# Feed-forward blocks of a two-stack transformer: up and down chunks interleaved, up chunks as seven products in every other iteration

## The chip, the cores and the metric

The kernel runs on one core of a Trainium2 chip. The metric is device time in microseconds (us) for one execution of the whole program. The engines of the core work in parallel, each with an in-order queue of its own: TensorE (PE, matmuls; PEld is its weight load), VectorE (DVE), ScalarE (ACT), GpSimd (POOL) and SyncE (SP), which here only issues DMAs. They wait for each other through semaphores.

## The reference

512 tokens of width 1024 pass through a first block (token mixers, memory attention, a feed-forward block with a convolution over the tokens) and two layers of a second block (feed-forward, mixer, feed-forward). The change is in the five feed-forward blocks (FFNs), which are

```python
def conv_ffn(n, w_up, conv_w, conv_b, w_down):       # FFN 0
    u, g = jnp.split(n @ w_up, 2, axis=-1)
    gp = jnp.pad(g, ((0, 0), (pad, pad), (0, 0)))
    gc = sum(gp[:, j:j + S] * conv_w[j] for j in range(CONV_WIDTH)) + conv_b
    return (jax.nn.silu(gc) * u) @ w_down

def swiglu(x, w_gate, w_up, w_down):                 # FFN 1 to 4
    return (jax.nn.silu(x @ w_gate) * (x @ w_up)) @ w_down
```

with `D_MODEL = 1024`, `D_FF = 2816`, all in float32. Each is applied to a normed input and its result, times 1.0 or 0.5, is added to the stream `h`.

## The kernel before

**Precision.** Every float32 product is made of three matmuls (L1995 to L1997, `products`): high part by high part, high weight by low input, low weight by high input. ScalarE makes the high part of a weight chunk (`split_hi`, L508, `w_hi` from `stage`), VectorE the low part (`split_lo`, L1002, `w_lo`). Activations are split in the same way (`x_hi`, `x_lo`; `f_hi`, `f_lo`).

**Chunks.** All weights come as one stream of chunks of 128 x 2048 values (1 MB), in the order in which TensorE uses them. `stage`, `w_hi` and `w_lo` have two slots each, for even and odd chunks. ScalarE splits chunk c + 2 when chunk c is done (`chunk_done`), VectorE follows (`lo_ready`), and SP loads chunk c + 4 into the slot that this frees. TensorE begins a chunk when its `lo_ready` and the evacuation of older PSUM tiles (`acc_evac`) are there.

**An FFN before.** The 2816 hidden columns are 22 tiles of 128, two to an iteration, so 11 iterations. Iteration `it` has a gate chunk (256 columns of w_gate) and an up chunk (256 of w_up). The iterations fall in three parts (`PARTS`: 4, 4 and 3 iterations); after each part come four chunks of w_down, each for 256 of the 1024 output columns with the part's 8, 8 or 6 tiles as the contraction. The tiles of gate, up and down lie in PSUM banks 0 to 3 in turn; banks 4 to 7 hold five of the products below.

**Eight and seven products.** A gate chunk is a 2 x 2 block product (contraction in halves, columns in two tiles, tokens in halves). As eight products it is 48 matmuls of 512 columns (`eight`). As seven products of sums (`seven_products`, a Strassen-Winograd scheme) it is 84 matmuls of 256 columns. For it VectorE makes four sums of the weights (`gate_sums`, `s_f`), ScalarE and VectorE split them (`s_hi`, L517; `s_lo`, L1012), and once an FFN four sums of the input: ScalarE scales (`t_half`), VectorE adds (`token_sums`, L1066 to L1071), both split (`t_hi`, `t_lo`). VectorE then puts the products together, in part while the chunk runs (`gate_early`, L1034 to L1043) and in part after it (`gate_evac`, L1054 to L1059). In FFN 0 the gates 4 to 10 are done so, in the others the gates 2 to 10. Up chunks are always eight products.

**VectorE's order in an iteration before.** It evacuates the gate (`gate_evac`; L1051 for eight products), splits the next gate chunk (`gate_lo(i, it + 1)`), does the convolution in FFN 0 (L1126 to L1130), then the token sums (all in iteration 0, in FFN 0 two each in iterations 0 and 1), evacuates the up tiles (L1140), splits the next up chunk, makes weight sums, `f_lo` (L1150) and the early part of the next gate. ScalarE applies silu (L576, L579) and makes `f_hi` (L561), GpSimd multiplies gate and up (L1873).

**Between FFNs.** `residual` adds the last four chunks of down to `h` (L1093) and makes `x_hi` (L544) and `x_lo` (L1099); GpSimd sums the squares (L1849, L1851). TensorE runs gate 0 of the next FFN, then a matmul with ones for the norm (L2035, for FFN 1 L2040), ScalarE takes the root (L531) and VectorE the reciprocal, `rstd` (L1080). Only then can gate 0 be evacuated, while TensorE runs up 0.

Of the kernel before, what the change touches and what calls it, by code (L numbers as in the profile page):

```python
# [19 lines left out]
F32 = mybir.dt.float32  # L20
# [7 lines left out]
P = 128  # L28
# [23 lines left out]
PARTS = [("a", 0, 4), ("b", 4, 4), ("c", 8, 3)]  # L52
SEVEN_FROM = [4, 2, 2, 2, 2]
NONE_OF = FT // 2


def _down_name(i, part):

    return f"down{i}" if part == "c" else f"down{i}{part}"


def _ffn(i):

    return [phase for part, _, n in PARTS for phase in ((f"up{i}{part}", 2 * n, 4 * n), (_down_name(i, part), 4, 8))]

# [66 lines left out]
def build(nc, stream, x_in, mem_in, pos_in, par_in, const_in, out):  # L132
    ctx = ExitStack()
    with ctx:
# [50 lines left out]
        snap = place("snap", ROPE, [P, 3, HALF])  # L185
# [103 lines left out]
        def sem(name):  # L289
# [24 lines left out]
        seven_done, seven_snap, seven_sum = sem("seven_done"), sem("seven_snap"), sem("seven_sum")  # L314
# [17 lines left out]
        side_landed, mem_sq_ready, side_stat, side_std, mem_n, mem_hi_ready, mem_ready = (  # L332
            sem("side_landed"), sem("mem_sq_ready"), sem("side_stat"), sem("side_std"), sem("mem_n"), sem("mem_hi_ready"), sem("mem_ready"))
# [54 lines left out]
        def nth(i, it):

            return sum(NONE_OF - first for first in SEVEN_FROM[:i]) + it - SEVEN_FROM[i]  # L390

        def gate_chunk(i, it):

            part, base, _ = PARTS[it // 4]
            return C0[f"up{i}{part}"] + 2 * (it - base), T0[f"up{i}{part}"] + 4 * (it - base)

        def seven_at(p, t=None):

            bank, half = PRODUCT[p] if p in PRODUCT else ((t + p - 3) % 4, 0)
            return ps[:, bank, HALF * half:HALF * half + HALF]  # L400
# [5 lines left out]
        T_GROUPS = {i: {0: [0, 1], 1: [2, 3]} if i == 0 else {0: [0, 1, 2, 3]} for i in range(5)}  # L406
        T_ROUND_AT = {i: 1 if i == 0 else 0 for i in range(5)}
# [89 lines left out]
        def _(act):  # L497
# [12 lines left out]
            def gate_hi(i, it):  # L510

                c, _ = gate_chunk(i, it)
                if not seven(i, it):
                    return split_hi((c, 0))
                split_hi((c, 0), SINGLES)
                act.wait_ge(s_sum, 4 * nth(i, it) + 4)
                act.activation(s_hi[:, :], s_f[:, :], ACT.Copy).then_inc(s_rounded, 1)  # L517

            def first_product(n):

                act.wait_ge(seven_done, 4 * n + 1)
# [11 lines left out]
            def residual(name):  # L533
# [3 lines left out]
                def step(it):  # L537
                    for pair in range(2):
                        split_hi((c0 + 2 + pair, it * 2))
# [11 lines left out]
                if name == "down4":  # L551
                    step(0)
                    step(1)
                else:
                    walk(act, 2, step)

            def ffn(i):

                def rounded(it, e):
                    act.wait_ge(prod_ready, FT * i + 2 * it + e + 1)  # L560
                    act.activation(f_hi[:, 2 * it % 8 + e, :], up_b[:, e, :], ACT.Copy).then_inc(f_hi_ready, 1)  # L561

                for part, base, count in PARTS:
                    end = base + count
                    for it in range(base, end):
                        c, t = gate_chunk(i, it)
                        if i == 1 and it == 1:
                            stat(NS0["renorm"])
                        if it + 1 < end:
                            gate_hi(i, it + 1)  # L570
                        else:
                            split_hi((c + 2, 0))
                        for e in range(2):
                            if i == 0:
                                act.wait_ge(conv_step, 6 * it + 3 * e + 3)
                                act.activation(gate_b[:, e, 1:1 + S], up_b[:, e, :], ACT.Silu).then_inc(silu_ready, 1)  # L576
                            else:
                                act.wait_ge(acc_evac, t + e + 1)
                                act.activation(gate_b[:, e, 1:1 + S], gate_b[:, e, 1:1 + S], ACT.Silu).then_inc(silu_ready, 1)  # L579
                        split_hi((c + 3, 0))  # L580
                        if it == T_ROUND_AT[i]:
                            act.wait_ge(t_sum, 16 * (i + 1))
                            for q in range(4):
                                act.activation(t_hi[:, q, :, :], t_f[:, q, :, :], ACT.Copy).then_inc(t_rounded, 1)
                        if it + 1 < end and seven(i, it + 1):
                            first_product(nth(i, it + 1))
                        rounded(it, 0)
                        rounded(it, 1)
                    if part != "c":
                        c = C0[_down_name(i, part)]  # L590
                        for j in range(4):
                            if j == 2:
                                gate_hi(i, end)
                            else:
                                split_hi((c + j + 2, 0))
                        if seven(i, end):
                            first_product(nth(i, end))
# [156 lines left out]
            def mem_rounded(a, b):  # L754
                for k in range(a, b):
                    act.wait_ge(mem_n, k + 1)
                    act.activation(mem_hi[:, k, :], mem_t[:, k % 2, :], ACT.Copy).then_inc(mem_hi_ready, 1)
# [232 lines left out]
        def _(dve):  # L990
# [14 lines left out]
            def gate_lo(i, it):  # L1005

                c, _ = gate_chunk(i, it)
                if not seven(i, it):
                    return split_lo((c, 0))
                split_lo((c, 0), SINGLES)  # L1010
                dve.wait_ge(s_rounded, nth(i, it) + 1)
                dve.tensor_tensor(s_lo[:, :], s_f[:, :], s_hi[:, :].bitcast(F32), ALU.subtract).then_inc(s_ready, 1)  # L1012

            def gate_sums(i, it):

                c, _ = gate_chunk(i, it)
                n, w = nth(i, it), KP * P
# [1837 lines left out]
```

## Time and profile before

| | |
|---|---|
| median of 3 runs | 2759.59 us (2759.25 to 2760.49) |
| the profiled execution | 2758.85 us, of which its span is 2757.0 us |
| TensorE busy | 2736.3 us, 99% of the span, 14384 matmuls |
| VectorE, ScalarE, GpSimd busy | 1827.6, 963.3 and 530.6 us |
| mean granted TensorE clock | 0.999 of full speed |

The profile is of one execution. Its page gives busy times by engine, a picture of the span in 40 slices, and the chain of work that ended last: here 95% TensorE. The queries of the trace give the waits of an engine by what released it, the groups of instructions by line and shape, stretches with their granted clock, and single instructions in order of time.

### The profile page before, as it was taken

What the parts mean: (1) busy time and instruction counts of PE and PEld (TensorE: products, weight loads), DVE (VectorE), ACT (ScalarE), POOL (GpSimd) and SP (SyncE); (2) the same over time, 40 slices, a digit from 0 to 9 for tenths busy, and PEclk for the clock granted to TensorE, in tenths of its full rate; (3) what the DMA queues carried; (4) which work ended last, traced back from release to release, by engine and by line L of the source; (5) the groups of instructions that cost most, each with busy time, mean ns of one, the idle gap of its engine ahead of it and who ended that gap; (6) DMA issues with size and microseconds to landing.
All of it is one profiled execution on the core that took longest, in us unless ns stands there. A gap on an engine that the chain in (4) does not pass through costs nothing.

```text
span 2757.0 us, 35919 instructions
## 1 busy us (share of the span) xinstructions
PE 2736.3 (99%) x14384; PEld 2340.8 (85%) x14384; DVE 1827.6 (66%) x2088; ACT 963.3 (35%) x1122; POOL 530.6 (19%) x364
## 2 busy tenths in 40 slices
PE   9999999999999999999999999999999999999999
PEld 7978889878888888988778889888898888888987
DVE  5778766558586885756575857568475665684754
ACT  4433533443232442323363423234232322242322
POOL 0124014041010452002223200023000142510100
PEclk9999999999999999999999999999999999999999
DMA  4212034223222323232302222322323233222232
GB/s 169 90 62 80 31 107 138 92 77 103 96 96 104 108 91 103 96 107 99 108 31 77 92 99 101 104 98 105 107 92 107 93 107 106 92 94 105 92 107 92
DMA packets 39748, 266.02 MB, mean 96 GB/s; under 512 B 4528, under 2 KB 5808, under 8 KB 8240
## 3 DMA queue, kind: packets, MB, share of 16 engines
q1 hardware_dynamic: 38016, 259.02, 27.5%
q10 hardware_dynamic: 1584, 4.87, 0.5%
q8 instruction: 113, 1.85, 0.3%
q14 instruction: 35, 0.29, 0.0%
HBM read 261.77 MB, written 2.10 MB: 96 GB/s over the span
## 4 chain that ended last, share of the span: by engine, by line
PE 95%; DVE 2%; ACT 1%; issue 1%; POOL 1%; DVEq 0%; POOLq 0%; ACTq 0%
PE ps L1995 30%; PE ps L1997 29%; PE ps L1996 29%; PE ps L2202 1%; DVE w_lo L1002 1%; PE ps L2268 1%; PE ps L2299 1%; ACT w_hi L508 1%; PE ps L2590 1%; PE ps L2562 1%; PE ps L2224 1%; PE ps L2282 0%; PE ps L2574 0%; PE ps L2035 0%; POOL up_b L1857 0%
## 5 line engine op out<-in xcount | busy, mean ns | idle before, releaser
L508 ACT ACTIVATE w_hi<-stage 128x2048 fp32r<-128x2048 f32 x241 | 443.5, 1840 | 1323.3 <-PE ps L1997 1321.1
L1995 PE MATMUL ps<-x_hi,w_hi 128*128 128x512 f32 (+1 forms) x2056 | 775.0, 377 | 0.0
L1996 PE MATMUL ps<-x_lo,w_hi 128*128 128x512 f32 (+1 forms) x2056 | 764.8, 372 | 0.0
L1997 PE MATMUL ps<-x_hi,w_lo 128*128 128x512 f32 (+1 forms) x2056 | 764.2, 372 | 0.0
L1002 DVE TENSOR_TENSOR w_lo<-stage,w_hi 128x2048 fp32r<-128x2048 f32 x241 | 580.8, 2410 | 103.1 <-ACT w_hi L508 103.1
L1995 PEld LDWEIGHTS ps<-x_hi,w_hi 128*128 128x128 f32 x2056 | 388.0, 189 | 69.6 <-issue 4.1
L1996 PEld LDWEIGHTS ps<-x_lo,w_hi 128*128 128x128 f32 x2056 | 388.2, 189 | 69.1 <-issue 3.9
L1997 PEld LDWEIGHTS ps<-x_hi,w_lo 128*128 128x128 f32 x2056 | 387.7, 189 | 68.0
L1873 POOL TENSOR_TENSOR up_b<-up_b,gate_b 128x512 f32<-128x512 f32 x110 | 132.1, 1222 | 1405.0 <-DVE up_b L1140 1405.0
L1995 PE MATMUL ps<-f_hi,w_hi 128*128 128x512 f32 x880 | 343.0, 390 | 2.2 <-DVE f_lo L1150 2.2
L1996 PE MATMUL ps<-f_lo,w_hi 128*128 128x512 f32 x880 | 342.5, 389 | 0.0
L1997 PE MATMUL ps<-f_hi,w_lo 128*128 128x512 f32 x880 | 342.3, 389 | 0.0
L1140 DVE TENSOR_TENSOR up_b<-ps,rstd 128x512 f32<-128x512 f32 x110 | 70.8, 686 | 198.6 <-PE ps L1997 198.5
L1995 PEld LDWEIGHTS ps<-f_hi,w_hi 128*128 128x128 f32 x880 | 165.2, 188 | 38.4 <-DVE f_lo L1150 4.3
L1997 PEld LDWEIGHTS ps<-f_hi,w_lo 128*128 128x128 f32 x880 | 165.2, 188 | 34.5
L1996 PEld LDWEIGHTS ps<-f_lo,w_hi 128*128 128x128 f32 x880 | 165.2, 188 | 34.1
L1164 DVE SCALAR_TENSOR_TENSOR h<-ps,h 128x512 f32<-128x512 f32 x80 | 51.5, 686 | 201.0 <-PE ps L1997 201.0
L1851 POOL TENSOR_TENSOR ssum<-ssum,sq 128x512 f32<-128x512 f32 x64 | 146.4, 2287 | 5.0
L1995 PE MATMUL ps<-t_hi,s_hi 128*128 128x256 f32 x516 | 146.0, 283 | 0.0
L1996 PE MATMUL ps<-t_lo,s_hi 128*128 128x256 f32 x516 | 146.0, 283 | 0.0
L1997 PE MATMUL ps<-t_hi,s_lo 128*128 128x256 f32 x516 | 146.0, 283 | 0.0
L1849 POOL TENSOR_TENSOR sq<-h 128x512 f32 x64 | 77.9, 1217 | 269.5 <-DVE h L1093 263.6
(441 smaller groups left out, 4102.6 us busy)
## 6 DMA issues: line engine op xcount, KB each, us to landing
stage<-in_stream SPq DMA_DIRECT2D x242, 1024.0 KB, 4.8
h<-in_x ACTq DMA_DIRECT2D x2, 1024.0 KB, 5.2
out_x<-h SPq DMA_DIRECT2D x8, 256.0 KB, 2.1
h<-in_x SPq DMA_DIRECT2D x6, 256.0 KB, 3.7
mem_raw<-in_mem ACTq DMA_DIRECT2D x1, 1024.0 KB, 4.7
stage<-in_stream SPq DMA_DIRECT2D x6, 128.0 KB, 4.5
h<-in_x SPq DMA_DIRECT2D x1, 512.0 KB, 5.3
mask_f<-in_constants ACTq DMA_DIRECT2D x1, 448.0 KB, 6.1
```

The lines of the kernel that those rows point to most:

```text
L508: act.activation(w_hi[slot][:, 0:width], stage[slot][:, 0:width], ACT.Copy).then_inc(hi_ready, 1)
L1002: dve.tensor_tensor(w_lo[slot][:, 0:width], stage[slot][:, 0:width], w_hi[slot][:, 0:width].bitcast(F32), ALU.subtract).then_inc(lo_ready, 1)
L1140: dve.tensor_tensor(up_b[:, e, :], ps[:, (t + 2 + e) % 4, :], rstd[:, :], ALU.mult).then_inc(acc_evac, 1)
L1164: dve.scalar_tensor_tensor(h[:, m, :], ps[:, (t + m) % 4, :], scale, h[:, m, :], ALU.mult, ALU.add).then_inc(acc_evac, 1)
L1849: pool.tensor_tensor(sq[:, :], row(h, m), row(h, m), ALU.mult).then_inc(sq_ready, 1)
L1851: pool.tensor_tensor(ssum[:, :], ssum[:, :], sq[:, :], ALU.add).then_inc(ss_ready, 1)
L1873: pool.tensor_tensor(up_b[:, e, :], up_b[:, e, :], gate_b[:, e, 1:1 + S], ALU.mult).then_inc(prod_ready, 1)
L1995: pe.matmul(out_ap, wh, xh, start=first, stop=False)
L1996: pe.matmul(out_ap, wh, xl, start=False, stop=False)
L1997: return pe.matmul(out_ap, wl, xh, start=False, stop=last)
L2202: mm = pe.matmul(ps[:, bank, b * P:(b + 1) * P], lhs, rhs, start=True, stop=True)
L2224: mm = pe.matmul(ps[:, 5 + 2 * e, :], QQ[e][:, 0, b * P:(b + 1) * P], A[e][:, b, :], start=(b == 0), stop=(b == BLK - 1))
```

## The change

It has these parts:

- An FFN is one phase of 30 chunks in the order gate 0, up 0, gate 1, up 1, gate 2, up 2, down 0, gate 3, up 3, down 1, and so on to gate 9, up 9, down 7, gate 10, up 10; then four tail chunks of down with the last 6 tiles as before. A down chunk inside covers four tiles of contraction and four of the eight output tiles (48 matmuls of 512 columns), and its result is added to `h` in one instruction.
- PSUM halves take turns: chunk p of the 30 uses banks 4 to 7 or 6 to 7 when p is even, 0 to 3 or 0 to 1 when it is odd. TensorE begins chunk p when chunk p - 2 is evacuated.
- In FFNs 1 to 4 the up chunks of iterations 2, 4, 6 and 8 are seven products too. In FFN 0 the gates are so from 3 on.
- The seven products are put together by five instructions after the chunk (`evacuated`); nothing of it is done during the chunk but a copy of the first product by ScalarE. A gate does its products with sums first, an up last, as `s_hi` and `s_lo` are single.
- VectorE, ScalarE and GpSimd handle the two tiles of an iteration in one instruction. The split of chunk p + 2 comes behind all of the work on chunk p's tiles, the convolution and the token sums included. In the last iteration `f_lo` comes before the split.
- The signs of the sums change, so that the four token sums of a tile are two dependent steps and two more, where one step waited before. The padding of the last down chunks is no longer split.

```diff
+def _order():
+    out = []
+    for it in range(STEPS):
+        out += [("gate", it), ("up", it)]
+        if 2 <= it < STEPS - 1:
+            out.append(("down", it - 2))
+    return out
+SEVENS = [{"gate": range(3, STEPS), "up": range(0)}] + 4 * [{"gate": range(2, STEPS), "up": range(2, STEPS - 1, 2)}]
...
-        T_GROUPS = {i: {0: [0, 1], 1: [2, 3]} if i == 0 else {0: [0, 1, 2, 3]} for i in range(5)}
+        T_SUMS = [{0: [0, 1], 2: [2, 3]}] + 4 * [{0: [0, 1, 2, 3]}]
...
 # VectorE
+            def evacuated(i, p, to):
+                if (i, p) not in NTH:
+                    b = two_banks(p)
+                    dve.tensor_tensor(to, ps[:, b:b + 2, :], free(rstd[:, :], 0, [[0, 2], [1, S]]), ALU.mult).then_inc(acc_evac, 2)
                     return
...
+                dve.tensor_tensor(blocks[:, 0:2, :], product(2, adjacent), free(first, 0, twice_dims), ALU.add).then_inc(blocks_sum, 1)
+                dve.wait_ge(blocks_sum, 4 * n + 1)
+                dve.tensor_tensor(blocks[:, 2, :], product(7, [[1, HALF]]), blocks[:, 1, :], ALU.add).then_inc(blocks_sum, 1)
+                dve.wait_ge(blocks_sum, 4 * n + 2)
+                dve.tensor_tensor(free(blocks[:, 1, :], 0, [[S, 2], [1, HALF]]), product(5, twice_dims), blocks[:, 1:3, :], ALU.add).then_inc(blocks_sum, 1)
+                dve.wait_ge(blocks_sum, 4 * n + 3)
+                dve.tensor_tensor(blocks[:, 1:3, :], product(3, adjacent), blocks[:, 1:3, :], ALU.add).then_inc(blocks_sum, 1)
+                dve.wait_ge(blocks_sum, 4 * n + 4)
+                dve.tensor_tensor(to, free(blocks[:, 0, :], 0, [[S, 2], [1, S]]), free(rstd[:, :], 0, [[0, 2], [1, S]]), ALU.mult).then_inc(acc_evac, 2)
...
+                for p, (kind, it) in enumerate(ORDER):
...
+                    dve.wait_ge(chunk_done, c + 1)
+                    if kind == "down":
...
+                        dve.scalar_tensor_tensor(h[:, m:m + 4, :], ps[:, b:b + 4, :], scale, h[:, m:m + 4, :], ALU.mult, ALU.add).then_inc(acc_evac, 4)
+                    elif kind == "gate":
+                        evacuated(i, p, gate_b[:, :, 1:1 + S])
                         if i == 0:
...
+                            convolved(it)
+                        for j in T_SUMS[i].get(p, []):
                             token_sums(i, j)
+                    elif it < STEPS - 1:
...
+                        evacuated(i, p, up_b[:, :, :])
...
+                    if kind_at(i, p + 2) == ("up", True):
+                        weight_sums(i, p + 2)
+                    ffn_lo(i, p + 2)
+                    if p == T_ROUND[i]:
+                        token_lo(i, 0)
+                        token_lo(i, 1)
...
+                    if kind_at(i, p + 3) == ("gate", True):
+                        weight_sums(i, p + 3)
+                    if kind == "up" and it < STEPS - 1:
+                        dve.wait_ge(f_hi_ready, f + 2)
+                        dve.tensor_tensor(f_lo[:, k:k + 2, :], up_b[:, :, :], f_hi[:, k:k + 2, :].bitcast(F32), ALU.subtract).then_inc(f_ready, 2)
...
 # TensorE
+            def clear(i, p):
+                c, t = chunk_at(i, p)
+                pe.wait_ge(lo_ready, c + 1)
+                pe.wait_ge(acc_evac, T0[f"up{i}"] + TILE_AT[p - 1] if p else t - 4)
...
+                clear(i, p)
+                pe.wait_ge(t_ready, 4 * (i + 1))
+                if kind == "gate":
+                    with_sums().then_inc(s_used, 1)
                 product(1, single(0, 0), tokens(0, 0))
+                product(2, single(1, 0), tokens(1, 0)).then_inc(first_done, 1)
+                mm = product(4, single(1, 1), token_sum(T4))
+                if kind == "up":
+                    mm = with_sums()
+                mm.then_inc(chunk_done, 1)
```

## Rows read from the trace of the kernel before

**Rows 1.** Page, part 1: busy us, share of the span, instructions.

```profile
PE 2736.3 (99%) x14384; PEld 2340.8 (85%) x14384; DVE 1827.6 (66%) x2088; ACT 963.3 (35%) x1122; POOL 530.6 (19%) x364
```

**Rows 2.** Waits of TensorE: waiter <- releaser, total us, times, longest.

```profile
PE ps L2040 <- POOL up_b L1857: 2.9, 1, 2.9
PE ps L1995 <- DVE f_lo L1150: 2.2, 5, 0.5
```

**Rows 3.** Timeline, ScalarE, L508: start us, us, what [idle before <- releaser].

```profile
1517.25 1.92 ACT L508 ACTIVATE w_hi<-stage 128x2048 fp32r<-128x2048 f32 x1 [7.74 <-PE ps L1997]
...
1539.94 1.92 ACT L508 ACTIVATE w_hi<-stage 128x2048 fp32r<-128x2048 f32 x1 [4.40 <-PE ps L1997]
1550.82 1.49 ACT L508 ACTIVATE w_hi<-stage 128x1536 fp32r<-128x1536 f32 x1 [1.80 <-PE ps L1997]
1561.70 1.91 ACT L508 ACTIVATE w_hi<-stage 128x2048 fp32r<-128x2048 f32 x1 [5.52 <-PE ps L1997]
1571.77 1.49 ACT L508 ACTIVATE w_hi<-stage 128x1536 fp32r<-128x1536 f32 x1 [5.84 <-PE ps L1997]
1582.68 1.92 ACT L508 ACTIVATE w_hi<-stage 128x2048 fp32r<-128x2048 f32 x1 [6.57 <-PE ps L1997]
...
1837.56 1.92 ACT L508 ACTIVATE w_hi<-stage 128x2048 fp32r<-128x2048 f32 x1 [7.94 <-PE ps L1997]
1846.45 1.92 ACT L508 ACTIVATE w_hi<-stage 128x2048 fp32r<-128x2048 f32 x1 [5.23 <-PE ps L1997]
```

**Rows 4.** Timeline, VectorE: a split beside GpSimd's product, FFN 2.

```profile
1563.65 3.12 DVE L1002 TENSOR_TENSOR w_lo<-stage,w_hi 128x2048 fp32r<-128x2048 f32 x1 [0.72 <-ACT w_hi L508]
```

**Rows 5.** Timeline, VectorE, start of FFN 2.

```profile
1533.10 1.29 DVE L1051 TENSOR_TENSOR gate_b<-ps,rstd 128x512 f32<-128x512 f32 x2
1534.30 2.28 DVE L1002 TENSOR_TENSOR w_lo<-stage,w_hi 128x2048 fp32r<-128x2048 f32 x1
1536.50 0.48 DVE L1066 SCALAR_TENSOR_TENSOR t_f<-h,par,t_f 128x256 f32<-128x256 f32 x1
...
1543.33 1.28 DVE L1140 TENSOR_TENSOR up_b<-ps,rstd 128x512 f32<-128x512 f32 x2
```

**Rows 6.** Timeline, all engines: TensorE restarts behind a late split.

```profile
579.85 2.33 DVE L1002 TENSOR_TENSOR w_lo<-stage,w_hi 128x2048 fp32r<-128x2048 f32 x1 [0.53 <-ACT w_hi L508]
...
582.23 0.50 PE L1995 MATMUL ps<-mo_hi,w_hi 128*128 128x512 f32 x1 [1.65 <-DVE w_lo L1002]
```

**Rows 7.** Timeline, VectorE and ScalarE, starts of FFN 0 and FFN 1.

```profile
620.18 1.29 DVE L1051 TENSOR_TENSOR gate_b<-ps,rstd 128x512 f32<-128x512 f32 x2
...
623.59 0.54 DVE L1126 TENSOR_SCALAR up_b<-gate_b,par 128x512 f32<-128x512 f32 x1
...
627.65 0.48 DVE L1066 SCALAR_TENSOR_TENSOR t_f<-h,par,t_f 128x256 f32<-128x256 f32 x1
...
637.91 1.92 ACT L508 ACTIVATE w_hi<-stage 128x2048 fp32r<-128x2048 f32 x1 [1.16 <-PE ps L1997]
...
959.46 1.92 ACT L508 ACTIVATE w_hi<-stage 128x2048 fp32r<-128x2048 f32 x1 [3.79 <-PE ps L1997]
...
978.79 1.29 DVE L1051 TENSOR_TENSOR gate_b<-ps,rstd 128x512 f32<-128x512 f32 x2
...
986.95 1.92 ACT L508 ACTIVATE w_hi<-stage 128x2048 fp32r<-128x2048 f32 x1 [5.71 <-PE ps L1997]
```

**Rows 8.** Timeline, TensorE, after the wait at the start of FFN 1.

```profile
974.87 0.63 PE L1996 MATMUL ps<-x_lo,w_hi 128*128 128x512 f32 x1
975.30 0.63 PE L1997 MATMUL ps<-x_hi,w_lo 128*128 128x512 f32 x1
```

**Rows 9.** Stretch: busy (count) of PE, PEld, DVE, ACT, POOL; PEclk, DMA, GB/s.

```profile
973.90:977.20 3.30, 3.30 (x8) 2.21 (x8) 1.80 (x1) 2.51 (x6) 2.96 (x4) 0.50 0.00 0
```

**Rows 10.** Groups by shape, VectorE: shapes, count | busy us, mean ns | idle before.

```profile
L1034 DVE TENSOR_TENSOR gate_b<-ps,snap 128x256 f32<-128x256 f32 x43 | 17.9, 417 | 0.0
...
L1566 DVE TENSOR_TENSOR qm<-ps,rstd 128x1024 f32<-128x1024 f32 x4 | 4.9, 1225 | 12.7 <-PE ps L1997 12.7
```

More of the change, by code:

```diff
@@ L51 @@
 KP = KT // 2
[L52 to L59, printed above, removed]
+STEPS = FT // 2
+def _order():
[5 more added lines that the diff above has]
+    return out
+ORDER = _order()
+TILES = {"gate": 2, "up": 2, "down": 4}
+TILE_AT = [sum(TILES[kind] for kind, _ in ORDER[:p]) for p in range(len(ORDER) + 1)]
+LAST_K = 4 * ((STEPS - 3) // 2)
+SEVENS = [{"gate": range(3, STEPS), "up": range(0)}] + 4 * [{"gate": range(2, STEPS), "up": range(2, STEPS - 1, 2)}]
 def _ffn(i):
-    return [phase for part, _, n in PARTS for phase in ((f"up{i}{part}", 2 * n, 4 * n), (_down_name(i, part), 4, 8))]
+    return [(f"up{i}", len(ORDER), TILE_AT[-1]), (f"down{i}", 4, 8)]
 PHASES = [
@@ L538, in step @@
                     for pair in range(2):
-                        split_hi((c0 + 2 + pair, it * 2))
+                        ahead = c0 + 2 + pair, it * 2
+                        split_hi(ahead, 3 * S if name.startswith("down") and it == 0 else CW)
                         for e in range(2):
@@ L557, in ffn @@
             def ffn(i):
[L559 to L570, printed above, removed]
-                        else:
[L572 to L597, printed above, removed]
@@ L1045, in gate_evac @@
[L1045 to L1059 removed]
+                dve.tensor_tensor(s4, a12, s2, ALU.subtract).then_inc(s_sum, 1)
@@ L1156, in ffn @@
[L1156 to L1174 removed]
+                                dve.wait_ge(silu_ready, f + 2)
@@ L1176, in first_piece @@
+                    if i == 1 and (kind, it) == ("gate", 1):
+                        dve.wait_ge(std_ready, NS0["renorm"] + 1)
+                        dve.reciprocal(sq[:, :], ssum[:, :]).then_inc(rstd_ready, 1)
             def first_piece(c, i):
@@ L2087, in token_sum, with product @@
                     return lambda j: (t_hi[:, q, j, :], t_lo[:, q, j, :])
-                def product(p, w, b):
+                def product(which, w, b):
+                    bank, half = PRODUCT[which]
                     for j in range(KP):
-                        mm = products(seven_at(p, t), w(j), b(j), j == 0, j == KP - 1)
+                        mm = products(ps[:, four_banks(p) + bank, HALF * half:HALF * half + HALF], w(j), b(j), j == 0, j == KP - 1)
                     return mm
-                begin(c, t, 2)
@@ new lines, in with_sums @@
+                def with_sums():
+                    pe.wait_ge(s_ready, n + 1)
+                    product(6, summed(S2), token_sum(T2))
+                    product(7, summed(S3), token_sum(T3))
+                    product(5, summed(S1), token_sum(T1))
+                    return product(3, summed(S4), tokens(1, 1))
+                clear(i, p)
+                pe.wait_ge(t_ready, 4 * (i + 1))
+                if kind == "gate":
+                    with_sums().then_inc(s_used, 1)
+                product(1, single(0, 0), tokens(0, 0))
```

378 lines of the change are left out of this document (193 added, 185 removed).

## Prediction

> **What bounds the kernel now.** I read the page first: its busy table gives TensorE 99% of the span [rows 1], so a microsecond comes off the end only if TensorE issues less or waits less. The waits of TensorE come second: the largest is 2.9 us at the start of FFN 1 (a sum on GpSimd), the next 2.2 us on `f_lo` in five pieces, one for each FFN [rows 2]. So TensorE's own work is the bound, and every other engine is paid for only where it makes TensorE wait. Third, the ScalarE rows of L508 are a clock for the chunks: each such row whose wait is on TensorE starts when a chunk is done. Between them a gate chunk as seven products (84 matmuls of 256 columns) takes 10.07 us and the up chunk behind it (48 of 512) 10.91 us; an eight-product chunk behind another is 10.88 us, all through the FFNs [rows 3]. That is 0.120 and 0.227 us for a matmul, with no wait between chunks.
>
> **The product count.** Before there are 43 seven-product chunks (7 in FFN 0, 9 in each of the others). After, FFN 0 has 8 and each other FFN has 9 gates and 4 ups: 60. Down work is the same (528 matmuls an FFN, now eight chunks of 48 and four of 36). A seven-product up saves 10.91 - 10.08 = 0.83 us, and the down chunk behind it costs 0.03 more, as the chunk behind a gate does now: 0.80 us. So 16 x 0.80 + 0.78 = **-13.6 us** on TensorE, which is all on the path.
>
> The Trainium skill ("TensorE: Matmul & The Clock Gate", section "Back-to-back issue gap") gives N/2.4 + 2.5 ns between matmuls, 109 and 216 ns for these two widths; by it a seven would save 1.19 us, all of them 20.2 us, and the forecast would be 6.6 us lower. The spacing that the rows of the chunks show differs from it, and the rows decide.
>
> **The wait on `f_lo` at the last step.** The first tail chunk of down takes 8.89 us where 36 matmuls need 36 x 0.227 = 8.16 [rows 3]. The cause is VectorE's order: after the last up it splits a weight chunk (3.1 us) before `f_lo`, beside GpSimd's product [rows 4]. The change puts `f_lo` ahead of that split. Then the last `f_lo` ends some 4.5 us after the up chunk (evacuations 1.3, GpSimd 2.2, ScalarE and VectorE 0.6 and 0.7), and TensorE needs it after 24 matmuls, 5.4 us. The wait goes: 4 x 0.73 + 0.61 = **-3.6 us**, with nothing late next.
>
> **The start of each FFN, where the change puts a wait in.** TensorE can begin gate 1 (the third chunk) only when `w_lo` of it is there. It now lies right behind the evacuation of gate 0, ahead of the token sums: evacuation at 1533.10, split at 1534.30, token sums from 1536.50, and the second chunk ends at 1539.94, 3.4 us after the split is done [rows 3, 5]. In the new `ffn` of VectorE `token_sums` runs inside the gate branch, and `ffn_lo(i, p + 2)` comes after it. Step by step for FFN 2: evacuation 1.20; token sums 4 x 1.78 = 7.1 (now 4 x 1.71 in 1536.50 to 1543.33 [rows 5]; the new order has two dependent steps where the old has one); split 2.28. Together 10.6 us: `w_lo` is done at 1543.7. TensorE issues the next chunk 0.26 us before the L508 row, so at 1539.68. A restart behind a late `w_lo` comes 0.05 us after it, at 582.23 against a split that ended at 582.18, and its first matmul takes 0.50 us; for it I add 0.09 [rows 6]. Loss 1543.70 + 0.14 - 1539.68 = 4.16 us. FFNs 3 and 4 repeat the pattern (the evacuation starts 6.84 us before the end of the second chunk in all three). FFN 0 has, ahead of the same split, the convolution (4.06) and two of the four token sums (3.56), with its evacuation at 620.18 and the second chunk's end 10.88 before 637.91, at 627.03 [rows 7]: 620.18 + 1.29 + 4.06 + 3.56 + 2.28 = 631.37, a loss of 4.74 us. FFN 1 evacuates at 978.79 and its second chunk ends at 986.95 [rows 7]: 989.39 + 0.14 - 986.69 = 2.84 us. FFN 0 has the other two token sums in step 2 and there 11.2 us of VectorE work ahead of a `w_lo` that TensorE wants after 10.6: 0.75 us. Sum 4.74 + 2.84 + 3 x 4.16 + 0.75 = **+20.8 us**. Behind the waiting gate 1 every matmul queues, as TensorE is in order; the DMA queue starts the load of gate 2 only when this split is done, but what reads that chunk first are its sums, behind four more instructions of the same VectorE queue. GpSimd and ScalarE have nothing due in that time.
>
> **The clock.** A stall can cost more than its length. After the wait of 2.9 us at the start of FFN 1 [rows 2] matmuls of 512 columns follow at 0.43 us instead of 0.227 [rows 8], and the granted clock of 973.90 to 977.20 is 0.50, the lower level of 1.2 GHz [rows 9]. From the last chunk of down to the end of the second chunk it is 27.49 us in FFN 1 and 22.69 in FFN 2 [rows 3, 7]: 4.8 us more, of which 2.9 are the wait, so 1.9 us are the clock. After the idle of 1.65 us before 582.23 even the first matmul takes 0.50 us [rows 6], less than the 0.63 of the lower level [rows 8]. The new waits in FFNs 0, 2, 3 and 4 leave 4.0 to 4.6 us idle, beyond the one that lost the clock; FFN 1's 2.7 us lies between the two rows. I take 4 falls x 1.9 = **+7.6 us**; the bounds are none and five of twice the length seen, 0 to +19.
>
> The same page of the Trainium skill (section "HAM oscillation — how this bites in real kernels") advises against longer idle gaps of TensorE for this reason. It speaks against this change, since it turns a kernel without such gaps in the FFNs into one with a gap in each; rows 8 and 9 agree, and by it the forecast stands while without it the sum would be 7.6 us lower.
>
> **The interleaved steady part, costed at nothing.** Per chunk VectorE has 10.1 or 10.9 us. The seven-product evacuation is now five dependent instructions after the chunk (three of 512 columns at half of 1.29, one of 256 at 0.42 and one of 1024 at 1.23, 3.6 us, and some 0.3 for four handovers: 3.9 us [rows 5, 10]) where part of it ran during the chunk before. Its cover is the PSUM half: the next chunk writes the other half, so the evacuation is due a whole chunk later. Tightest steps: after a seven-product up, 3.9 + `s_lo` 2.3 + split 1.8 to 2.7 = 8.0 to 8.9, due at 10.6; after a down ahead of a seven-product up, 2.5 + sums 2.7 + split 1.8 = 7.0, due at 9.8, and `s_lo` then waits for the gate's summed products (48 x 0.12 = 5.8 us, then ScalarE 1.9) and ends 10.1 us into the gate chunk, where the up wants it 4.3 us later. In FFN 0 a seven-product gate has 3.9 + 4.1 (convolution) + 2.3 = 10.3 ahead of the split of down, due at 10.6: 0.3 us to spare, eight times. A split beside GpSimd takes 3.1 instead of 2.28 us [rows 4, 5]; GpSimd's product now falls behind the up evacuation as before. If the cover is gone, 1 us at each of 16 sevens and 8 gates is the upper bound; below nothing is excluded, as there are no waits there to remove. Merged instructions (two tiles in one) shorten VectorE's queue by 0.1 us each and are worth nothing.
>
> **The sum.** -13.6 - 3.6 + 20.8 + 7.6 = +11.2 us. The profiled execution took 2758.85 us (span 2757.0 and 1.85 around it), 0.74 below the median of 2759.59. So 2770.1 for it, 2770.8 for the median; I give 2771.
>
> **Rivals.**
> - The clock stays up (chance 0.18). The stalls are as computed, but 4 us of idle don't bring the level down, or only once. For it: after 1.65 us of idle nothing fell. Against: 2.89 us did it. +3.6 us, 2763.
> - TensorE doesn't wait at the start of an FFN (0.09), the one on the other side: VectorE reaches the split of gate 1 in time. It needs the 10.6 us from rstd to `w_lo` to be under 6.6. For it: in the trace of before nobody waits there. Against: the order in the diff, and the token sums' rows. -17.2 us, 2742. From 2.3 us a start instead of 4.2, with the clock up, the kernel would be faster by over 0.2%.
> - The interleaved part stalls as well (0.13): VectorE's evacuation chain after a seven-product up or, in FFN 0, behind the convolution holds the next split. For it: 0.3 us to spare in FFN 0. Against: over 1.5 us elsewhere. Half of the bound, some 10 us more: 2781.
>
> **How the numbers follow.** The forecast has 0.60. The range 2761 to 2781 takes in the first rival, half of the third and the bounds of the clock up to twice 1.9 for four falls; the second rival stays outside. A difference of 0.2% (5.5 us) is about what a measurement of this kernel can tell from no change. Slower by more: forecast and third rival, nearly all: 0.71. Within: the first rival and the low end of the forecast: 0.20. Faster: 0.09.
>
> **What would show it.** In the waits of TensorE a row on `w_lo`, five times with up to about 4.3 us, and the row on `f_lo` gone; in the windows behind these waits a granted clock of 0.50 for some 3 us; chunk ends 10.08 us apart for seven-product ups; 0.7 us less before the first tail chunk. I am wrong if gate 1 follows without a wait, if the clock is 1.00 behind it, or if waits on `w_lo`, `s_lo` or `h` show up past the third chunk of an FFN.

## The result and the profile after

The changed kernel takes 2777.27 us (median of 4 runs, 2776.68 to 2777.96); the kernel before, run beside it, 2759.73 (2759.25 to 2760.49). The ratio is 1.0065, interval [1.0053, 1.0077]: 17.5 us slower, where +11.2 was forecast; the time lies inside the range of 2761 to 2781. The profiled execution took 2777.96 us with a span of 2776.2, 19.2 us more span than before; the accounts below are made against that.

The page of after: its busy table, and of the costliest groups the one with the new idle time.

```profile
PE 2732.0 (98%) x14996; PEld 2364.4 (85%) x14996; DVE 1986.5 (72%) x1917; ACT 978.1 (35%) x1051; POOL 550.2 (20%) x314
...
L2023 PE MATMUL ps<-x_hi,w_hi 128*128 128x512 f32 (+1 forms) x1920 | 711.6, 371 | 23.7 <-DVE w_lo L1024 22.9
```

The waits of TensorE in after (waiter <- releaser, total us, times, longest):

```profile
PE ps L2023 <- DVE w_lo L1024: 27.8, 10, 4.6
...
PE ps L2068 <- POOL up_b L1880: 1.5, 1, 1.5
```

TensorE issues 612 matmuls more than before and is busy 4.3 us less [rows 1]: narrower matmuls, so the products did come down. Against [rows 2], the row on `f_lo` is gone, the one on GpSimd has fallen from 2.9 to 1.5 (no run takes apart why), and a row on `w_lo` of 27.8 us is new (1.6 of it was there before). The timeline of TensorE, the first matmul behind each of these waits (start, us, what, [idle before <- releaser]):

```profile
631.96 0.79 PE L2023 MATMUL ps<-x_hi,w_hi 128*128 128x512 f32 x1 [4.60 <-DVE w_lo L1024]
...
657.28 0.50 PE L2023 MATMUL ps<-x_hi,w_hi 128*128 128x512 f32 x1 [0.52 <-DVE w_lo L1024]
...
995.14 0.50 PE L2023 MATMUL ps<-x_hi,w_hi 128*128 128x512 f32 x1 [3.84 <-DVE w_lo L1024]
...
1032.12 0.38 PE L2023 MATMUL ps<-x_hi,w_hi 128*128 128x256 f32 x1 [2.35 <-DVE w_lo L1024]
...
1044.83 0.50 PE L2023 MATMUL ps<-f_hi,w_hi 128*128 128x512 f32 x1 [2.38 <-DVE w_lo L1024]
1056.88 0.39 PE L2023 MATMUL ps<-t_hi,s_hi 128*128 128x256 f32 x1 [0.88 <-DVE w_lo L1024]
...
1556.32 0.80 PE L2023 MATMUL ps<-x_hi,w_hi 128*128 128x512 f32 x1 [3.87 <-DVE w_lo L1024]
...
1911.64 0.80 PE L2023 MATMUL ps<-x_hi,w_hi 128*128 128x512 f32 x1 [3.87 <-DVE w_lo L1024]
...
2443.35 0.71 PE L2023 MATMUL ps<-x_hi,w_hi 128*128 128x512 f32 x1 [3.88 <-DVE w_lo L1024]
```

Six of the nine are the forecast ones: gate 1 of each FFN, and gate 2 of FFN 0. The three from 1032.12 to 1056.88, all in FFN 1, are not in the forecast. VectorE at the start of FFN 2 shows the first kind, to be laid beside [rows 5]: evacuation of gate 0, sixteen instructions of token sums (the first and the last stand here), and only then the split.

```profile
1545.76 1.23 DVE L1065 TENSOR_TENSOR gate_b<-ps,rstd 128x1024 f32<-128x1024 f32 x1
1546.90 0.47 DVE L1090 SCALAR_TENSOR_TENSOR t_f<-h,par,t_f 128x256 f32<-128x256 f32 x1
...
1553.58 0.48 DVE L1095 SCALAR_TENSOR_TENSOR t_f<-h,par,t_f 128x256 f32<-128x256 f32 x1
1553.98 2.28 DVE L1024 TENSOR_TENSOR w_lo<-stage,w_hi 128x2048 fp32r<-128x2048 f32 x1
```

The split ends at 1556.26; the second chunk had ended at 1552.54. Behind it, two stretches (us, then busy of PE, PEld, DVE, ACT, POOL, PEclk, DMA, GB/s), the first in FFN 2, the second in FFN 3:

```profile
1556.30:1559.60 3.30, 3.28 (x8) 2.63 (x9) 3.30 (x3) 1.94 (x3) 2.03 (x1) 0.53 0.67 196
1911.90:1917.20 5.30, 5.30 (x13) 4.14 (x14) 5.30 (x3) 1.99 (x3) 3.89 (x1) 0.50 0.77 238
```

The clock is at its lower level, 1.2 GHz, until 1559.4 in the one and 1917.8 in the other (by stretches of 1 us), so for 3.1 and 6.2 us behind TensorE's restart, though the waits ahead are both 3.87 us. Last, the chunk ends on ScalarE (the L508 rows of [rows 3], now L525), in FFN 2 and in FFN 1:

```profile
1552.54 1.91 ACT L525 ACTIVATE w_hi<-stage 128x2048 fp32r<-128x2048 f32 x1 [3.12 <-PE ps L2025]
...
1579.93 1.49 ACT L525 ACTIVATE w_hi<-stage 128x1536 fp32r<-128x1536 f32 x1 [6.64 <-PE ps L2025]
1590.00 1.92 ACT L525 ACTIVATE w_hi<-stage 128x2048 fp32r<-128x2048 f32 x1 [1.11 <-PE ps L2025]
...
1610.99 1.92 ACT L525 ACTIVATE w_hi<-stage 128x2048 fp32r<-128x2048 f32 x1 [1.82 <-PE ps L2025]
```

```profile
1019.80 1.49 ACT L525 ACTIVATE w_hi<-stage 128x1536 fp32r<-128x1536 f32 x1 [4.70 <-PE ps L2025]
...
1067.32 1.92 ACT L525 ACTIVATE w_hi<-stage 128x2048 fp32r<-128x2048 f32 x1 [1.07 <-PE ps L2025]
```

In FFN 2 gate 1 and up 1 take 27.39 us instead of 21.76 (two chunks of 10.88): 4.1 for the wait, 1.5 for the clock. Gate 2 takes 10.07, and the next pair (up 2 of seven products, down 0) 20.99, one after the other to the end of the FFN: the steady part runs as forecast. Gate 2, up 2, down 0 and gate 3 together take 41.13 us when nothing waits; in FFN 1 these four chunks take 47.52, so 6.4 us are lost there.

### The profile page after: what moved, and what is told of

Read it like the earlier page. It is cut to its first block, busy times and chain, and to the rows that moved or that the text cites. A ratio compares the mean times of both kernels' runs of the same rounds, so it can differ in the third digit from the quotient of the medians.

```text
span 2776.2 us, 36914 instructions
## 1 busy us (share of the span) xinstructions
PE 2732.0 (98%) x14996; PEld 2364.4 (85%) x14996; DVE 1986.5 (72%) x1917; ACT 978.1 (35%) x1051; POOL 550.2 (20%) x314
## 4 chain that ended last, share of the span: by engine, by line
PE 92%; DVE 5%; ACT 1%; issue 1%; POOL 1%; DMA 0%; SPq 0%; DVEq 0%; POOLq 0%; ACTq 0%
PE ps L2023 29%; PE ps L2024 29%; PE ps L2025 28%; DVE w_lo L1024 1%; PE ps L2253 1%; PE ps L2319 1%; PE ps L2350 1%; PE ps L2641 1%; PE ps L2613 1%; PE ps L2275 1%; DVE rstd L1104 0%; DVE t_f L1092 0%; PE ps L2333 0%; ACT w_hi L525 0%; POOL sq L1872 0%
## 5 line engine op out<-in xcount | busy, mean ns | idle before, releaser
L2023 PE MATMUL ps<-x_hi,w_hi 128*128 128x512 f32 (+1 forms) x1920 | 711.6, 371 | 23.7 <-DVE w_lo L1024 22.9
L2024 PE MATMUL ps<-x_lo,w_hi 128*128 128x512 f32 (+1 forms) x1920 | 700.7, 365 | 0.0
L2025 PE MATMUL ps<-x_hi,w_lo 128*128 128x512 f32 (+1 forms) x1920 | 700.1, 365 | 0.0
L525 ACT ACTIVATE w_hi<-stage 128x2048 fp32r<-128x2048 f32 (+1 forms) x241 | 426.7, 1770 | 709.5 <-PE ps L2025 707.2
L1024 DVE TENSOR_TENSOR w_lo<-stage,w_hi 128x2048 fp32r<-128x2048 f32 (+1 forms) x241 | 548.1, 2274 | 42.2 <-ACT w_hi L525 42.2
L2023 PEld LDWEIGHTS ps<-x_hi,w_hi 128*128 128x128 f32 x1920 | 365.2, 190 | 85.5 <-DVE w_lo L1024 25.7
L1901 POOL TENSOR_TENSOR up_b<-up_b,gate_b 128x1024 f32<-128x1024 f32 x50 | 140.8, 2817 | 1261.8 <-DVE up_b L1065 811.4
L542 ACT ACTIVATE s_hi<-s_f 128x2048 fp32r<-128x2048 f32 x60 | 115.1, 1918 | 291.1 <-PE ps L2025 247.5
L2025 PE MATMUL ps<-t_hi,s_lo 128*128 128x256 f32 x720 | 203.8, 283 | 0.0
L2024 PE MATMUL ps<-t_lo,s_hi 128*128 128x256 f32 x720 | 203.7, 283 | 0.0
L1037 DVE TENSOR_TENSOR s_lo<-s_f,s_hi 128x2048 fp32r<-128x2048 f32 x60 | 169.6, 2826 | 38.8 <-ACT s_hi L542 38.8
```

Of the source, the lines that this page charges most:

```text
L525: act.activation(w_hi[slot][:, 0:width], stage[slot][:, 0:width], ACT.Copy).then_inc(hi_ready, 1)
L1024: dve.tensor_tensor(w_lo[slot][:, 0:width], stage[slot][:, 0:width], w_hi[slot][:, 0:width].bitcast(F32), ALU.subtract).then_inc(lo_ready, 1)
L1901: pool.tensor_tensor(up_b[:, :, :], up_b[:, :, :], gate_b[:, :, 1:1 + S], ALU.mult).then_inc(prod_ready, 2)
L2023: pe.matmul(out_ap, wh, xh, start=first, stop=False)
L2024: pe.matmul(out_ap, wh, xl, start=False, stop=False)
L2025: return pe.matmul(out_ap, wl, xh, start=False, stop=last)
```

## The experiments

All times are beside runs of the kernel before on the same chip, which gave 2758.8 to 2759.5 us. In the text "sums" are the weight sums for a seven-product chunk (`s_f`), "split" is `w_lo`.

**The split ahead of the token sums.** Only the place of one call changes, in the gate steps:

```
                         evacuated(i, p, gate_b[:, :, 1:1 + S])
+                        ffn_lo(i, p + 2)
...
                         weight_sums(i, p + 2)
-                    ffn_lo(i, p + 2)
+                    if kind != "gate":
+                        ffn_lo(i, p + 2)
```

> The changed kernel with one edit: in every gate step VectorE splits chunk p + 2 right behind the evacuation, ahead of the convolution and the token sums. My theory: the waits of TensorE for w_lo at gate 1 (22.0 us in all, with the 0.8 us at gate 2 of FFN 0) and the half clock behind them (10.8 us) go, so 2777.3 - 32.8 = 2744 to 2747 us, faster than the kernel before; the 6.4 us that FFN 1 loses between gate 2 and gate 3 stay. Rival, the interleaving itself costs (five evacuation steps behind each seven-product chunk, PSUM halves): then the time stays above 2755 us and waits appear in the later steps of FFNs 0, 2, 3 and 4. Rival, the waits only move to another engine or to the next chunk: near 2777 us.

Measured: 2751.5 us (2750.0 to 2752.1, 9 runs), ratio 0.9971 [0.9961, 0.9981]. The waits at the starts are gone, and with 25.7 us less than the changed kernel this is the main cause, shown. But it is 4.5 to 7.5 us above what was expected, and its waits say where:

```profile
PE ps L2025 <- DVE w_lo L1024: 6.8, 4, 2.5
PE ps L2025 <- DVE t_lo L1100: 2.9, 4, 0.9
```

The `t_lo` row is the split of the token sums, which is now due at gate 2: 0.7 to 0.9 us in each of FFNs 1 to 4. The `w_lo` row is FFN 1 again (1.6 of it was there before). The four chunks of FFN 1 take 51.23 us, so 10.1 are lost, more than the 6.4 of the changed kernel: 6.0 us of waits (0.88 on `t_lo`; 0.26, 2.38 and 2.51 on `w_lo`), and two falls of the clock that the changed kernel does not have there. The `w_lo` waits in the stretch did not grow (5.2 us against 5.6); what came on top is `t_lo` and the two falls, some 1.7 us each. The stretches behind the two longer waits:

```profile
1030.00:1034.00 4.00, 4.00 (x13) 3.19 (x12) 4.00 (x3) 0.00 (x0) 3.84 (x3) 0.65 0.77 260
1045.00:1048.00 3.00, 3.00 (x14) 3.00 (x15) 3.00 (x2) 1.28 (x1) 0.00 (x0) 0.50 0.62 177
```

**The same late split in the kernel before.** In an iteration with token sums, `gate_lo(i, it + 1)` moves from behind the evacuation of the gate to behind the token sums:

```
                         gate_evac(i, it)
-                        if it + 1 < end:
+                        late = it in T_GROUPS[i]
+                        if it + 1 < end and late:
+                            pass
+                        elif it + 1 < end:
                             gate_lo(i, it + 1)
...
                             token_sums(i, j)
+                        if late:
+                            gate_lo(i, it + 1)
```

> The kernel before with one edit: in the iterations with token sums VectorE splits the next gate chunk behind the convolution and the token sums, as the change does. Theory: the order alone makes the loss at the start of the FFNs: 3.9 us in FFNs 2 to 4, 2.6 in FFN 1, 4.6 and 0.4 in FFN 0, together 19.2 us, and 5 to 12 us of half clock behind four or five of them: 2784 to 2791 us. Rival: without the interleaved order and the PSUM halves the late split is hidden, 2759 to 2762 us.

Measured: 2787.5 us, ratio 1.0104. The waits, and the first matmul of gate 1 in FFN 1:

```profile
PE ps L2000 <- DVE w_lo L1002: 19.2, 7, 4.3
```

```profile
997.40 0.50 PE L2000 MATMUL ps<-x_hi,w_hi 128*128 128x512 f32 x1 [2.23 <-DVE w_lo L1002]
```

The one move, without any interleaving, costs 28 us. So the loss belongs to the place of this call and not to the new order of the chunks. In FFN 1 the wait is 2.23 us where FFNs 2 to 4 have 3.63; this kernel still has the wait of 2.89 us on GpSimd and the fall of the clock behind it, ahead of that place.

**TensorE kept busy through the wait.** Fourteen matmuls of 512 columns into a PSUM bank that nothing reads, ahead of gate 1:

```
+                    if p == 2:
+                        for _ in range(14):
+                            pe.matmul(ps[:, 2, :], x_hi[:, 0, 0:P], x_hi[:, 0, :], start=True, stop=True)
```

> The changed kernel with 14 matmuls of 512 columns more (3.2 us, into a PSUM bank that nothing reads) ahead of gate 1 in each FFN, in the time in which TensorE waits for w_lo. They add no wait; they only take the idle of some 4 us down to under 1 us. Theory, the clock falls because TensorE is idle for so long: the granted clock stays 1.00 behind gate 1, 10.8 us less, 2765 to 2769 us. Rival, the slow stretch has another cause than idleness (loads of weights from slots that VectorE and GpSimd write, the restart itself): 2776 to 2779 us, or more by what the added matmuls cost.

Measured: 2767.9 us (2767.2 to 2768.2), 9.4 less than the changed kernel, with the mean clock at 0.999 instead of 0.995. The stretch behind the wait in FFN 2 now has a clock of 1.00:

```profile
1552.00:1556.00 4.00, 3.92 (x17) 3.25 (x18) 4.00 (x4) 2.01 (x3) 2.67 (x1) 1.00 0.67 229
```

TensorE does more work and the kernel is faster: the time lost to the clock behind these waits is real, and is 9.4 us by the medians and 10.2 by the spans of the two profiled executions. The split comes as late as before. All of the difference lies at the starts: in FFN 1 gate 2 to gate 3 take 47.51 us against 47.52, though there the clock fell once behind a wait of 2.37 us, since the waits are shorter by about as much.

**GpSimd made light in FFN 1.** In the trace of after and in the kernel with the early split, GpSimd scales the residual stream `h` for the last norm in FFN 1 and multiplies it by the norm's factor, eight tiles each, just where the unforeseen waits are. Here both passes work on 8 of the 512 tokens; the kernel leaves out the rest of that norm:

```
-                            pool.tensor_scalar(h[:, m, :], h[:, m, :], pc("final_norm", m), None, ALU.mult).then_inc(renormed, 1)
+                            pool.tensor_scalar(h[:, m, 0:8], h[:, m, 0:8], pc("final_norm", m), None, ALU.mult).then_inc(renormed, 1)
...
-                            pool.tensor_tensor(h[:, m, :], h[:, m, :], sq[:, :], ALU.mult).then_inc(renormed, 1)
+                            pool.tensor_tensor(h[:, m, 0:8], h[:, m, 0:8], sq[:, 0:8], ALU.mult).then_inc(renormed, 1)
```

> The changed kernel with GpSimd's scaling and norm of h in FFN 1 done on 8 of the 512 tokens only (it leaves out that part of the first block's final norm). Theory: the waits for w_lo at up 2, down 0 and gate 3 of FFN 1 come from VectorE's weight sums and splits taking 1.7 to 3.4 us instead of 0.7 to 2.3 beside GpSimd's 37 us of work; they go, 6.4 us less, 2770 to 2772 us, while the wait at gate 1 of each FFN stays. Rival: VectorE's queue is late there by its own length (the reciprocal of 3.3 us, seven-product evacuations of 3.9 us), the waits stay and the time is 2776 to 2778 us.

Measured: 2771.7 us, 5.6 less, as expected. The same edit on the kernel with the early split:

> The kernel with the split ahead of the conv block (2751.5 us), in which GpSimd's two passes over the residual stream in FFN 1 (the scaling by the last norm's weight and the product with the norm's factor) work on 8 of 512 tokens; that part of the last norm is left out of the output. Theory: GpSimd beside VectorE is the cause of FFN 1's loss of 10.1 us: 2741 to 2743 us, the sums at 0.7 us instead of 1.8. Rival: the position of the sums alone makes VectorE late: 2746 to 2751 us.

Measured: 2742.6 us, 9.0 less. The four chunks take 42.08 us, which is 41.13 and the 0.9 for `t_lo`. VectorE in that stretch, first with GpSimd's full passes, then with the light ones:

```profile
1013.34 3.56 DVE L1024 TENSOR_TENSOR w_lo<-stage,w_hi 128x1536 fp32r<-128x1536 f32 x1
1016.83 3.39 DVE L1037 TENSOR_TENSOR s_lo<-s_f,s_hi 128x2048 fp32r<-128x2048 f32 x1
1020.14 2.32 DVE L1196 TENSOR_TENSOR f_lo<-up_b,f_hi 128x1024 fp32r<-128x1024 f32 x1
1022.38 0.68 DVE L1075 TENSOR_TENSOR blocks<-ps,ssum 128x512 f32<-128x512 f32 x1
...
1029.53 1.78 DVE L1050 TENSOR_TENSOR s_f<-stage 128x512 f32<-128x512 f32 x1
```

```profile
1013.50 1.76 DVE L1024 TENSOR_TENSOR w_lo<-stage,w_hi 128x1536 fp32r<-128x1536 f32 x1
1015.57 2.29 DVE L1037 TENSOR_TENSOR s_lo<-s_f,s_hi 128x2048 fp32r<-128x2048 f32 x1 [0.31 <-ACT s_hi L542]
1017.77 1.23 DVE L1196 TENSOR_TENSOR f_lo<-up_b,f_hi 128x1024 fp32r<-128x1024 f32 x1
1018.92 0.68 DVE L1075 TENSOR_TENSOR blocks<-ps,ssum 128x512 f32<-128x512 f32 x1
...
1024.96 0.68 DVE L1050 TENSOR_TENSOR s_f<-stage 128x512 f32<-128x512 f32 x1
```

And GpSimd's row beside the first of the two, and beside the second:

```profile
1015.25 18.90 POOL L1912 TENSOR_TENSOR h<-h,sq 128x512 f32<-128x512 f32 x8
```

```profile
1011.66 7.68 POOL L1912 TENSOR_TENSOR h<-h,sq 128x8 f32<-128x8 f32 x8
```

Beside GpSimd's full pass, or the product of gate and up just ahead of it (1013.01 to 1015.29), the instructions whose two inputs lie in SBUF take 1.1 to 1.8 us more each; `blocks<-ps,ssum`, with one input in PSUM, takes 0.68 us in both. With three slowed instructions of a sum on top of slowed splits, VectorE is late. The Trainium skill ("GPSIMD Engine Reference", section "Specifications") says that GpSimd's SBUF interfaces are shared with VectorE, with contention where a VectorE instruction has two SBUF inputs; these rows agree, the PSUM one too; beside GpSimd's other pass the contention is small, and there the measurement decides.

By the rows it is the second of GpSimd's two passes that does it; no run makes only one of them light. In the changed kernel, the scaling (one tensor in) with a split beside it, and the multiplication (two tensors in) with three rows beside it:

```profile
1000.34 19.57 POOL L1905 TENSOR_SCALAR h<-h,par 128x512 f32<-128x512 f32 x8
1014.12 1.75 DVE L1024 TENSOR_TENSOR w_lo<-stage,w_hi 128x1536 fp32r<-128x1536 f32 x1
```

```profile
1025.31 17.32 POOL L1910 TENSOR_TENSOR h<-h,sq 128x512 f32<-128x512 f32 x8
1025.82 1.78 DVE L1053 TENSOR_TENSOR s_f<-s_f,stage 128x512 f32<-128x512 f32 x1
1031.98 3.39 DVE L1037 TENSOR_TENSOR s_lo<-s_f,s_hi 128x2048 fp32r<-128x2048 f32 x1
1035.30 2.31 DVE L1194 TENSOR_TENSOR f_lo<-up_b,f_hi 128x1024 fp32r<-128x1024 f32 x1
```

No VectorE instruction that meets the scaling alone takes over 0.6 us more than without it. The product of gate and up, which every iteration has for 2 to 4 us, slows splits to some 3.6 us in all FFNs, but only one or two instructions meet it.

**No sums in that stretch.** The list of seven-product chunks alone changes, for FFN 1 (gates from 3, ups from 4):

```
+SEVENS = ... + [{"gate": range(3, STEPS), "up": range(4, STEPS - 1, 2)}] + 3 * [{"gate": range(2, STEPS), "up": range(2, STEPS - 1, 2)}]
```

> The kernel with the split ahead of the conv block (2751.5 us), and in FFN 1 alone the seven-product chunks begin later: gates from 3, ups from 4, so that no weight sum lies in the stretch in which GpSimd scales the residual stream. Two chunks become eight products (+1.6 us). Theory: FFN 1's loss of 10.1 us between its gate 2 and gate 3 comes from VectorE's weight sums running beside GpSimd, and without the sums there the plain splits fit even beside GpSimd: 2743 us (2741 to 2746). Rival: the plain splits of the weights and activations, slowed beside GpSimd, are late on their own: the loss stays at 3 us or more, 2747 to 2753 us.

Measured: 2743.3 us (2742.7 to 2743.4), ratio 0.9944 [0.9927, 0.996]. GpSimd works in full here, and still 8.2 us go, 1.6 of eight-product chunks paid. `w_lo` waits are down to the 1.6 us that the kernel before has too. So it takes both: the sums, and GpSimd beside them.

**No up chunk as seven products.** First on the kernel with the early split:

```
-... + 4 * [{"gate": range(2, STEPS), "up": range(2, STEPS - 1, 2)}]
+... + 4 * [{"gate": range(2, STEPS), "up": range(0)}]
```

> The kernel with the split ahead of the conv block (2751.5 us), and no up chunk as seven products in FFN 1 to 4, so 16 chunks go back to eight products. By the count alone it is slower by 16 x 0.80 = 12.8 us: 2764 us. Theory of FFN 1 (the sums of gate 3 and up 2 meet GpSimd's work): without up 2's sums part of the 10.1 us loss goes, some 3 to 8 us: 2756 to 2761 us. Rival, that the splits alone are late there: 2764 us, and FFN 1's loss unchanged.

Measured: 2757.0 us, 5.4 more instead of 12.8. The missing 7.4 us are FFN 1's: gate 2 to gate 3 take 44.50 us there, 2.6 over the 41.93 of one eight-product chunk more, against 10.1. The other three FFNs pay the full 3.2 us each. The same edit on the changed kernel, so the new order alone:

> The changed kernel with no up chunk as seven products: the interleaved order and its later splits alone, one gate chunk of FFN 0 as seven products more than before. The 16 up chunks at 0.80 us go back to eight products, +12.8 us on 2777.3; FFN 1's loss of 6.4 us between gate 2 and gate 3 goes by 4 to 6.4 us, since up 2 brings no weight sums there: 2784 to 2786 us, so 25 to 27 us slower than before. The prediction's own terms without those 16 chunks (-0.8, -3.6, +20.8, +7.6) give 2783.5 us. Rival: the order costs something in every pair of chunks that the up sevens happened to cover: over 2790 us.

Measured: 2783.9 us (2782.2 to 2784.2), ratio 1.0088 [1.0071, 1.0105], against the 2783.5 of the prediction's own terms; `w_lo` waits of 22.2 us in 7, so no more than the starts of the FFNs have. Per pair of up and down 21.79 us, 10.91 and 10.88: interleaving by itself costs nothing in the steady part. Nor is anything lost in FFN 1, where up 1 ends and gate 3 ends 41.93 us apart:

```profile
1019.49 1.91 ACT L525 ACTIVATE w_hi<-stage 128x2048 fp32r<-128x2048 f32 x1 [4.71 <-PE ps L2025]
...
1061.42 1.92 ACT L525 ACTIVATE w_hi<-stage 128x2048 fp32r<-128x2048 f32 x1 [1.07 <-PE ps L2025]
```

GpSimd works in full here and the sums of gate 3 are made too, so the 6.4 us of the changed kernel need the sums of up 2.

**All up chunks as seven products.** On the kernel with the early split, `"up": range(2, STEPS - 1)` in FFNs 1 to 4, 16 chunks more:

> The kernel with the split of the next gate chunk ahead of the conv block (2751.5 us), and in FFN 1 to 4 the up chunks as seven products in every iteration from 2 to 9 instead of every other one: 16 chunks more. Theory: the interleaved part has room on VectorE, so 16 chunks x 0.80 us come off and little else changes: 2738 to 2742 us, FFN 1's loss growing by up to 2 us for the added weight sums of its up 3 beside GpSimd. Rival: VectorE's queue is full with two sums a chunk in both gate and up, so that splits of weights come late in every iteration: 2750 us or more, with many short waits of TensorE on the split of the weights in FFN 2 to 4.

Measured: 2738.9 us (2737.4 to 2739.4), ratio 0.9928 [0.9912, 0.9945], 12.6 less. VectorE goes to 77% of the span, and the waits on `w_lo` stay at 6.8 us in 4. The last of them, 2.52 us long, left the clock at 1.00 here, so the profiled execution has one fall in FFN 1 where the kernel with the early split has two.

**All of it together**, with FFN 1 from gate 3 and up 4:

> Both of the other two edits on the kernel with the split ahead of the conv block (2751.5 us): up chunks as seven products in every iteration from 2 to 9 of FFN 2 to 4 and from 4 to 9 of FFN 1, gates of FFN 1 from 3. Against that kernel 14 chunks more and 2 fewer as seven products, one of them an up chunk and one a gate chunk: net 13 x 0.80 = 10.4 us come off, and FFN 1's 10.1 us of loss as well: 2731 us (2729 to 2735). Rival of a full VectorE: 2740 us or more.

Measured: 2731.3 us (2731.0 to 2731.5), ratio 0.990 [0.9884, 0.9917]. This beats both kernels, by 28 and 46 us. It has 468 matmuls more than the kernel with the early split, so 13 seven-product chunks more (15 added, 2 taken back; the "14 chunks more" of the expectation is a slip, its net of 13 is not). Its busy table, its waits, and the stretch in FFN 1 in which TensorE had waited:

```profile
PE 2709.4 (99%) x15464; PEld 2371.1 (87%) x15464; DVE 2073.7 (76%) x2034; ACT 1001.9 (37%) x1077; POOL 577.0 (21%) x314
```

```profile
PE ps L2025 <- DVE t_lo L1100: 2.0, 3, 0.7
PE ps L2187 <- DVE sq L1208: 1.8, 1, 1.8
PE ps L2025 <- DVE w_lo L1024: 1.6, 1, 1.6
```

```profile
1004.00:1060.00 56.00, 56.00 (x288) 48.09 (x287) 37.79 (x27) 16.13 (x12) 23.82 (x14) 1.00 0.27 95
```

## Why the prediction was right, and where it fell short

Sign and range hold; the sum is short by 8.0 us against the profiled span (19.2 measured, 11.2 forecast), and by 6.3 us against the medians. Two of its terms were too small, and one that was put at nothing was not. Step by step:

- **The product count**, -13.6: right. Chunk ends are 10.07 us apart for seven products and 20.99 for a seven-product up with its down, 0.80 less than 21.79. Sixteen chunks more later gave 12.6 us, 0.79 each. The formula of the Trainium skill ("TensorE: Matmul & The Clock Gate", section "Back-to-back issue gap"), which the page gives for the gap of a matmul by itself and not for a stream, makes it 1.19 us a chunk, an estimate, and 19 for the sixteen; the runs decide against it.
- **The wait on `f_lo`**, -3.6: right (its terms add up to 3.53). No such row is left, and the tail chunks are 8.16 us apart.
- **The start of each FFN**, +20.8: measured 22.0, from the waits above (20.6) with some 0.2 us for each slower first matmul. FFNs 0, 2, 3 and 4 are within 0.2 us of the forecast, and gate 2 of FFN 0 took 0.81 for 0.75. FFN 1's term was mis-sized: 4.1 for 2.84. The 8.16 us between evacuation and second chunk end [rows 7] held the fall of the clock behind the wait on GpSimd; in after that fall is gone, TensorE arrives sooner, and the distance is 6.8 us as in the others. One stall had been hiding part of the next: in the kernel before with the late split, where the first stall is still there, FFN 1 waits 2.23 us and not 3.84.
- **The clock**, +7.6: mis-sized. There are five falls, not four, since FFN 1's wait came out long enough; they cost 2.9, 1.7, 1.5, 3.0 and 1.7 us, 10.8 together, and the old one of 1.9 is gone: +8.9. The kernel with filler matmuls puts the falls at the starts at 9.4 to 10.2. That the price was real, against the first rival, is shown; that it would be 1.9 each time is not so.
- **The interleaved steady part, costed at nothing**: this step failed, in one place. In FFN 1 it costs 6.4 us. "Over 1.5 us elsewhere" was worked out with VectorE's durations from stretches in which GpSimd does one short product. The stretch in which GpSimd works on `h` for some 37 us was not costed. There the sums of up 2, behind a reciprocal of 3.34 us, fall into the 17 us of its multiplication and take 1.7 to 2.5 us an instruction instead of 0.7, between splits that take 3.4 instead of 2.3. The trace of before does show such splits beside GpSimd [rows 4]; they cost nothing there, as there was no up with sums. Everywhere else the step was right, FFN 0 with its 0.3 us of room too, eight times.
- **The wait on GpSimd** was left at 2.9 us and is 1.5, -1.4: a small gain that the prediction did not look for.

22.0 + 8.9 + 6.4 - 1.4 - 13.6 - 3.6 = 18.7 of the 19.2 us.

Of the rivals, the first fell by the filler kernel, the second by the waits themselves. The third (the interleaved part stalls as well) is half right: it named the seven-product evacuation in every step, or FFN 0's convolution, and it was neither, but a VectorE slowed by GpSimd in one FFN.

Not settled: why behind waits of the same length the clock stays at its lower level for 3.1 us here and 6.2 us there. The traces show what goes with it. Over 25 falls behind waits, in eight of the kernels, the low stretch is either 3.4 or 6.8 us long; the nine long ones began 0.7 to 2.0 us before TensorE's restart, the sixteen short ones from 0.3 us before it to 1.5 us behind it. What decides when a fall begins they do not show. With the early split it also stays open how much of FFN 1's loss is due to gate 3's sums: without up 2's 7.5 of the 10.1 us go, but then an eight-product chunk also gives VectorE 0.8 us.

## What to carry to other kernels

When a step is re-ordered, list on the engine that serves the bound one everything between the evacuation and the next split: one call moved past 7 us of work that nobody needed yet made 22 us of waits and 9 of lost clock, more than the saved products, and moving it back made a gain of the whole change. Where an in-order engine has little room, read its durations from the stretch where its neighbour works longest, not from the usual one. And look at what a stall hides: with one gone, TensorE arrives sooner and the next wait is longer (2.23 us with the wait on GpSimd and its fall of the clock ahead of it, 3.84 without the fall). A loss further on can grow as well (6.4 to 10.1 us), here by a clock that now fell where it had not and by a split that became due.

## What the hardware showed that was not expected

- A wait of 2.35 or 2.38 us in FFN 1 of the changed kernel left the clock at 1.00; one of 2.38 us and one of 2.51 with the early split brought it down to 0.50, one of 2.37 did so in the kernel with filler matmuls, and one of 2.52 with all up chunks as seven products left it at 1.00. In after and in all the kernels made from it the wait of 1.51 us on GpSimd did nothing, where 2.89 us in before did [rows 9]. Length alone does not decide for waits of 2.3 to 2.6 us.
- A fall costs 1.5 or 3.0 us at the same place: FFN 2 lost 1.5 and FFN 3 3.0 in the changed kernel; with the new order alone FFN 2 took 28.77 us for gate 1 and up 1, and FFN 3 27.54, the other way round.
- A VectorE subtraction of 128x1536 from two SBUF inputs takes 1.76 us alone and up to 3.56 beside a GpSimd instruction with two inputs; an addition of 128x512 takes 0.68 alone and 1.7 to 2.5 beside one; with an input in PSUM it stays at 0.68. Beside GpSimd's scaling, with one tensor in, the same kinds take 0 to 0.6 us more.
- Filler matmuls that nothing reads made the kernel 9.4 us faster while TensorE was busy 7.0 us longer.
